# Sixteen experts: gate and up as seven block products instead of eight, on the two column halves of the array

## The chip, the cores and the metric

The kernel runs on one core of one Trainium2 chip. The metric is the device time of one launch in microseconds (us). Before the change the median of three runs is 3734.11 us (3731.77 to 3739.34).

The engines are TensorE (PE; its weight loads are listed as PEld), VectorE (DVE), ScalarE (ACT), GpSimd (POOL) and SyncE (SP), which here issues most DMAs. Data lie in SBUF (the one large tensor `arena`); matmuls write to PSUM (`ps`, eight banks of 512 words in each of 128 partitions).

## The reference, cut to what matters

The program computes a hybrid layer and then a second layer. The change is in the mixture of experts of the first layer:

```
def expert_choice_ffn(h, w_router, w_gate, w_up, w_down):
    def route_set(t):                       # t: 1024 tokens x 1024
        n = t.shape[0]
        cap = CAP_FACTOR * n // N_EXPERTS   # 128 tokens for each of 16 experts
        aff = jax.nn.softmax((t @ w_router).astype(jnp.float32), axis=-1)
        gate, idx = lax.top_k(aff.T, cap)
        xe = t[idx]
        hid = jax.nn.silu(jnp.einsum('ecd,edf->ecf', xe, w_gate)) * jnp.einsum('ecd,edf->ecf', xe, w_up)
        ye = jnp.einsum('ecf,efd->ecd', hid, w_down) * gate[..., None].astype(t.dtype)
        return jnp.zeros_like(t).at[idx.reshape(-1)].add(ye.reshape(-1, t.shape[-1]))
```

Each expert has three 1024 x 1024 matrices of float32, 12.6 MB together, and multiplies 128 tokens by each.

## The kernel before

The program is a row of stages with a barrier between them. `stage_choose` finds each expert's 128 tokens on VectorE and meanwhile loads the weights of expert 0. `stage_experts` (line 1757 on) does the experts one after the other. There is no scheduler: each engine has its instructions in the order of the code and waits on semaphores that the code names.

A weight matrix lies in two halves of four k blocks (`W[n][:, half]`, 2 MB each, loaded by one DMA), one buffer for each matrix. So a half of the next expert can be loaded as soon as TensorE has gone past that half (`load`, L1800).

TensorE's order for expert i (`body`, L1861) is: gate half 0, the eight transposes of the hidden rows of expert i-1 (`turn(hid)`), gate half 1, down of expert i-1 (two halves), the eight transposes of the tokens of expert i+1 (`turn(xe)`), up (two halves). A half is eight matmuls in the code, with 128 tokens as the stationary operand and 512 columns of weights as the moving one; a float32 matmul is two records in the trace. So an expert takes 96 records of 128x512 and 16 of 128x128, all on the full array, written `128*128` in the rows.

ScalarE copies the turned tokens out of PSUM (`rows_in`) and does silu (`gate`). VectorE multiplies (`hidden`, L1922), copies the turned hidden rows (L1928) and scales the result (L1936, `y`). GpSimd gathers the tokens (L1817, an indirect DMA from `h_scratch`) and adds `y` to the output rows (L1822, an indirect DMA to `x_scratch`). At the stage's start it also makes two products of gains for a later stage (L1829, L1831), which need `final_g` and `norm1_g_2`. SyncE issues the loads of these two (L1797, L1798) behind fourteen small loads for a later stage (L1787 to L1795).

A later stage, `stage_ffn_up` (L3210), already multiplies by seven block products on the full array; it has sums of operands on GpSimd (L3247 to L3250) and VectorE (L3315 to L3319).

## Time and profile before

| | |
|---|---|
| median of three runs | 3734.11 us |
| the profiled execution | 3731.01 us |
| its span, first to last instruction | 3729.1 us |
| TensorE busy | 3453.5 us (93%) |
| granted TensorE clock, mean | 0.963 |
| VectorE, ScalarE, GpSimd busy | 41%, 20%, 15% |
| mean HBM traffic | 114 GB/s |

All durations below come from that one profiled execution. PE busy counts a matmul to its modelled end, so two matmuls in a row overlap: the time that a stream of them costs is read from the distance of their starts. The clock is 1.00 at 2.4 GHz and 0.50 at 1.2 GHz. A row such as `PE L1845 MATMUL ... 128*128 128x512 f32 x48` merges 48 records; the first pair of numbers is the part of the array used (rows by columns), the second the shape of the result. In brackets stands how long the engine was idle before, and who ended it.

### The profile page before, as it was taken

How to read it: one execution, taken by the hardware profiler on the slowest of the kernel's cores; microseconds unless marked ns; L12 is line 12 of the kernel's file. 1: busy time of each engine (PE TensorE's matmuls, PEld its weight loads, DVE VectorE, ACT ScalarE, POOL GpSimd, SP SyncE). 2: the span in 40 equal slices, each digit the busy share in tenths (PEclk: the TensorE clock that was granted, in tenths of full speed). 3: DMA queues.
4: the chain of work that ended last, by engine and by line, in shares of the span. 5: the costliest groups of instructions: out<-in, count | busy, mean ns of one | idle time of the engine just before them, and what ended most of it. 6: DMA issues, size and time to landing. Idle time of an engine off the chain costs nothing. (4 is left out here: it accounts for less than half of the span.)

```text
span 3729.1 us, 32988 instructions
## 1 busy us (share of the span) xinstructions
PE 3453.5 (93%) x12660; PEld 1795.2 (48%) x12660; DVE 1524.8 (41%) x2809; ACT 748.1 (20%) x1454; POOL 559.9 (15%) x437
## 2 busy tenths in 40 slices
PE   6999999986889499999996989899999999999999
PEld 3445665545755244444443565345444444444444
DVE  3526853666343400000007658999322322211510
ACT  2004542442421000000002222233311101101000
POOL 0003420025610000000000020134200222221000
PEclk8999999998999699999997999999999999999999
DMA  6400001033332698888854033112223111110400
GB/s 245 146 23 23 1 2 34 24 106 91 82 137 95 242 339 315 315 316 322 318 189 165 0 59 96 51 38 91 95 70 115 34 45 45 45 35 28 152 23 34
DMA packets 199714, 427.59 MB, mean 115 GB/s; under 512 B 71449, under 2 KB 125881, under 8 KB 186753
## 3 DMA queue, kind: packets, MB, share of 16 engines
q1 hardware_dynamic: 190146, 394.18, 30.6%
q0 software_dynamic: 8272, 29.38, 2.6%
q8 instruction: 92, 1.51, 0.2%
q10 hardware_dynamic: 1152, 2.10, 0.2%
q14 instruction: 52, 0.43, 0.0%
HBM read 380.56 MB, written 43.88 MB: 114 GB/s over the span
## 5 line engine op out<-in xcount | busy, mean ns | idle before, releaser
L1845 PE MATMUL psum<-arena 128*128 128x512 f32 x1536 | 669.2, 594 | 2.5 <-DVE arena L1928 1.3
L3258 PE MATMUL psum<-arena 128*128 128x512 f32 x1232 | 534.1, 596 | 4.3 <-DVE arena L3316 3.3
L1845 PEld LDWEIGHTS psum<-arena 128*128 128x128 f32 x1536 | 289.0, 190 | 359.9 <-issue 356.9
L3258 PEld LDWEIGHTS psum<-arena 128*128 128x128 f32 x1232 | 235.5, 191 | 302.2 <-issue 296.8
L3412 PE MATMUL psum<-arena 128*128 128x512 f32 x528 | 229.6, 597 | 3.6 <-PEq L3231 3.6
L750 PE MATMUL psum<-arena 128*128 128x512 f32 (+1 forms) x512 | 198.3, 540 | 1.1 <-PEq L460 1.1
L2883 PE MATMUL psum<-arena 128*128 128x512 f32 x416 | 191.7, 604 | 3.7 <-ACT arena L2945 3.3
L2389 DVE TENSOR_SCALAR_CACHE_REDUCE arena<-arena 128x1024 f32<-128x1024 f32 (+2 forms) x192 | 173.6, 943 | 2.6 <-PEq L2462 0.8
L3412 PEld LDWEIGHTS psum<-arena 128*128 128x128 f32 x528 | 100.7, 191 | 132.5 <-issue 132.3
L2972 POOL TENSOR_SCALAR arena<-arena 128x128 f32<-128x128 f32 (+7 forms) x64 | 112.9, 1776 | 326.7 <-DVE arena L3008 326.7
L2133 PE MATMUL psum<-arena 128*128 128x512 f32 (+1 forms) x384 | 161.9, 581 | 0.0
L474 POOL TENSOR_TENSOR arena<-arena 128x1280 f32<-128x1280 f32 x32 | 92.6, 2894 | 423.9 <-DVE arena L589 423.9
L3327 DVE TENSOR_TENSOR arena<-arena,psum 128x512 f32<-128x512 f32 x44 | 30.3, 689 | 306.8 <-PE psum L3258 306.8
L1936 DVE SCALAR_TENSOR_TENSOR arena<-psum,arena 128x1024 f32<-128x1024 f32 x16 | 20.6, 1286 | 308.4 <-PE psum L1845 308.4
L750 PEld LDWEIGHTS psum<-arena 128*128 128x128 f32 x512 | 95.5, 189 | 91.0 <-issue 87.8
L355 PE MATMUL psum<-arena 128*128 128x512 f32 (+1 forms) x320 | 127.7, 554 | 1.9 <-PEq L154 1.9
L2133 PEld LDWEIGHTS psum<-arena 128*128 128x128 f32 x384 | 88.7, 233 | 68.5 <-issue 55.5
L3247 POOL TENSOR_TENSOR arena<-arena 128x512 f32<-128x512 f32 x22 | 28.6, 1299 | 611.0 <-PE psum L3258 370.8
L2883 PEld LDWEIGHTS psum<-arena 128*128 128x128 f32 x416 | 75.7, 192 | 92.2 <-issue 87.1
L1922 DVE TENSOR_TENSOR arena<-arena,psum 128x1024 f32<-128x1024 f32 x16 | 19.6, 1223 | 240.2 <-PE psum L1845 240.2
L1602 PE MATMUL psum<-arena 128*128 128x512 f32 x256 | 114.4, 602 | 2.2 <-PEq L1461 2.2
L3144 PE MATMUL psum<-arena 128*128 128x512 f32 x256 | 110.9, 592 | 2.4 <-PEq L3046 2.4
(513 smaller groups left out, 4635.0 us busy)
## 6 DMA issues: line engine op xcount, KB each, us to landing
arena<-in_w_gate_dram SPq DMA_DIRECT2D x32, 2048.0 KB, 7.4
arena<-in_w_up_dram SPq DMA_DIRECT2D x32, 2048.0 KB, 9.2
arena<-in_w_down_dram SPq DMA_DIRECT2D x32, 2048.0 KB, 8.2
arena<-in_w_mod_dram SPq DMA_DIRECT2D x12, 2048.0 KB, 9.7
arena<-gd_rows SPq DMA_DIRECT2D x56, 256.0 KB, 4.2
arena<-in_w_in_dram SPq DMA_DIRECT2D x22, 512.0 KB, 4.5
arena<-in_w_ffn_gate_dram SPq DMA_DIRECT2D x11, 1024.0 KB, 5.4
arena<-in_w_ffn_up_dram SPq DMA_DIRECT2D x11, 1024.0 KB, 5.3
```

Source lines behind the costliest of these rows:

```text
L355: ins = nc.tensor.matmul(e.ps[:, i % 4, 0:n], w[:, c % 2, k, m * P:(m + 1) * P], e.hT[:, k, s:s + n], start=(k == 0), stop=(k == KD - 1))
L474: nc.gpsimd.tensor_tensor(pr[:, i % SLOTS, 0], pr[:, i % SLOTS, 0], pr[:, i % SLOTS, 1], ALU.add).then_inc(s_comb, 1)
L750: ins = nc.tensor.matmul(e.ps[:, i % 4, 0:n], w[:, (m // 2) % 2, k, (m % 2) * P:(m % 2 + 1) * P], e.hT[:, k, s:s + n], start=(k == 0), sto ...
L1602: ins = nc.tensor.matmul(ps[:, 2 * (t % 2) + j, :], cat(k)[:, t * P:(t + 1) * P], w[:, k, j * 512:(j + 1) * 512], start=(k == 0), stop=(k ...
L1845: ins = nc.tensor.matmul(ps[:, banks + j, :], lhs[:, k], W[n][:, h, k % 4, j * 512:(j + 1) * 512], start=(k == 0), stop=(k == KD - 1))
L2133: ins = nc.tensor.matmul(ps[:, BANK(i), 0:n], lhs, w[:, (c + 2) % 3, k, 0:n], start=(k == 0), stop=(k == KD - 1))
L2389: ins = nc.vector.tensor_scalar(junk[j][:, 0:b.shape[-1]], b, cand.bitcast(F32)[:, j:j + 1], 0.0, ALU.is_ge, ALU.add, accum_out=count[:, j ...
L2883: ins = nc.tensor.matmul(ps[:, 7, :], wg[:, c % 2, k], hT[:, k, n * 512:(n + 1) * 512], start=(k == 0), stop=(k == KD - 1))
L2972: nc.gpsimd.tensor_scalar(v, v, sm[:, k % 2, 0, m:m + 1], None, ALU.mult).then_inc(s_nm, 1)
L3144: ins = nc.tensor.matmul(ps[:, 2 * (t % 2) + j, :], e.merged[:, k, t * P:(t + 1) * P], w[:, k, j * 512:(j + 1) * 512], start=(k == 0), sto ...
L3258: ins = nc.tensor.matmul(out(q), left[:, k], right[:, k], start=first and k == 0, stop=last and k == 3, skip_group_check=not first)
L3412: ins = nc.tensor.matmul(ps[:, bank + t, :], left(c)[:, tok(t)], right(c), start=first and c == 0, stop=c == KC - 1, skip_group_check=not ...
```

## The change

Gate and up are each multiplied as 2 x 2 blocks by the Winograd form of Strassen's scheme, which needs seven block products for eight. The tokens are split into two halves of 64 (`m`) and the contraction into the two weight halves (`h`); the weights' columns are split into quarters `b11, b12, b21, b22` that take four of every eight words. A product (`product`) has 64 tokens as the stationary operand, so it fills half of the array's columns; the code issues gate's matmul into PSUM partitions 0 to 63 and up's into 64 to 127, one after the other, for each of four k blocks. Down stays as it was.

The sums of weights (`t1` to `t4`, 128 x 2048 words each) are made by VectorE for gate and by GpSimd for up: `t3 = b22 - b12` in place of `b12` once both halves of the matrix are there (`third`), `t2 = t3 + b11` and `t1 = b22 - t2` after product P7, `t4 = b21 - t2` after P3. The semaphores `s_tg` and `s_tu` count them. VectorE makes four sums of tokens (128 x 256). Three partial results are put together by VectorE (`t[:, 0..2]`, six operations of 128 x 512), after ScalarE has copied four of them out of PSUM (`kept`); then TensorE transposes the four tiles (16 transposes, `tiles_turned`), and silu and the product with up are done on the transposed tiles. The loads of expert i+1 wait for the sums now, in the order gate 0, up 0, gate 1, up 1. `xe` has one buffer instead of two. (`...`: lines left out.)

```diff
+    t = A.take("tiles", 4, 512)
+    T = {n: [A.take(f"sum_{n}{m}", 4, 512) for m in range(3)] for n in ("gate", "up")}
...
+    xe = A.take("xe", D)
...
+    y = e.rows[:, 0]
...
+    X, Y, Z, V = range(4)
+    P1, P7, P2, P3, P6, P5, P4 = range(1, 8)
+    quarter = lambda n, h, c: W[n][:, h].rearrange("p k (m c) -> p k m c", c=KD)[:, :, :, 4 * c:4 * c + 4]
+    spread = lambda v: v.rearrange("p (m c) -> p m c", c=4)
+    b11, b12, b21, b22 = ({n: quarter(n, h, c) for n in ("gate", "up")} for h in range(2) for c in range(2))
+    t1, t2, t4 = ({n: T[n][m].rearrange("p k (m c) -> p k m c", c=4) for n in ("gate", "up")} for m in range(3))
+    t3 = b12
+    s3, s1, s2, s4 = (S[:, m] for m in range(4))
+    tokens = lambda b, h, m: xT[:, b, 4 * h:4 * h + 4, 64 * m:64 * m + 64]
...
+            def load(n, h, i):
+                sp.dma_start(W[n][:, h], src[n][bass.ds(i, 1), :, 4 * h:4 * h + 4, :].rearrange("a p k n -> p (a k) n")).then_inc(s_w[n][h], 16)
+
+            def body(i, b, first=False, second=False, last=False):
+                if not last:
+                    sp.wait_ge(s_tg, 4 * i + 2)
+                    load("gate", 0, i + 1)
+                    sp.wait_ge(s_tu, 4 * i + 2)
+                    load("up", 0, i + 1)
+                    sp.wait_ge(s_tg, 4 * i + 4)
+                    load("gate", 1, i + 1)
+                    sp.wait_ge(s_tu, 4 * i + 4)
+                    load("up", 1, i + 1)
+                if not first:
+                    for h in range(2):
+                        sp.wait_ge(s_d, 2 * i + h - 1)
+                        load("down", h, i)
+
+            experts(sp, body)
...
+            def third(i):
+                for h in range(2):
+                    pool.wait_ge(s_w["up"][h], 16 * (i + 1))
+                TT(t3["up"], b22["up"], b12["up"], ALU.subtract).then_inc(s_tu, 1)
...
-            gather(1)
...
             nc.gpsimd.tensor_tensor(e.rows[:, 1], e.rows[:, 1], e.rows[:, 1], ALU.mult).then_inc(e.s_gains, 1)
+            third(0)
+            pool.wait_ge(s_xt, 1)
+            gather(1)
             for i in range(NE):
-                if 1 <= i < NE - 1:
-                    gather(i + 1)
+                pool.wait_ge(s_mm, 7 * i + P7)
+                pool.wait_ge(s_tu, 4 * i + 1)
+                TT(t2["up"], t3["up"], b11["up"], ALU.add).then_inc(s_tu, 1)
+                pool.wait_ge(s_tu, 4 * i + 2)
+                TT(t1["up"], b22["up"], t2["up"], ALU.subtract).then_inc(s_tu, 1)
+                pool.wait_ge(s_mm, 7 * i + P3)
+                TT(t4["up"], b21["up"], t2["up"], ALU.subtract).then_inc(s_tu, 1)
                 if i:
+                    if i >= 2:
+                        pool.wait_ge(s_out, 16 * (i - 1))
                     scatter(i - 1)
+                if i + 2 < NE:
+                    pool.wait_ge(s_xt, i + 2)
+                    gather(i + 2)
+                if i + 1 < NE:
+                    third(i + 1)
+            pool.wait_ge(s_out, 16 * (NE - 1))
             scatter(NE - 1)
+            pool.wait_ge(s_out, 16 * NE)
...
+            def product(bank, left, right, first, last):
+                for k in range(4):
+                    for m, n in enumerate(("gate", "up")):
+                        ins = nc.tensor.matmul(spread(ps[64 * m:64 * m + 64, bank, :]), left[:, k], right[n][:, k], start=first and k == 0, stop=last and k == 3,
+                                               skip_group_check=not first)
+                ins.then_inc(s_mm, 1)
...
+            def tiles_turned():
+                for bank, pair in ((6, (t[:, 3], t[:, 1])), (4, (t[:, 0], t[:, 2]))):
+                    for c in range(2):
+                        for k in range(4):
+                            ins = nc.tensor.transpose(ps[:, bank + c, k * P:(k + 1) * P], pair[c].rearrange("p (m k) -> p k m", k=4)[:, k], e.ident)
+                    ins.then_inc(s_ct, 1)
...
+            def sums(i, n):
+                pe.wait_ge(s_tg, 4 * i + n)
+                pe.wait_ge(s_tu, 4 * i + n)
...
+                pe.wait_ge(s_xT, i + 1)
+                for n in ("gate", "up"):
+                    pe.wait_ge(s_w[n][0], 16 * (i + 1))
...
+                    pe.wait_ge(s_ev, 4 * i)
+                product(X, a11, b11, True, True)
                 if not first:
-                    pe.wait_ge(s_sg, i)
-                half("gate", 0, x, i, 0)
+                    pe.wait_ge(s_c, 6 * i)
+                    if not second:
+                        pe.wait_ge(s_y, i - 1)
+                    tiles_turned()
+                sums(i, 1)
+                pe.wait_ge(s_xs, 4 * i + 1)
+                product(Y, s3, t3, True, True)
+                for n in ("gate", "up"):
+                    pe.wait_ge(s_w[n][1], 16 * (i + 1))
+                pe.wait_ge(s_ev, 4 * i + 1)
+                product(X, a12, b21, False, True)
+                pe.wait_ge(s_xs, 4 * i + 4)
+                product(Z, s4, b22, True, True)
...
+                    down(i - 1)
+                sums(i, 2)
+                pe.wait_ge(s_ev, 4 * i + 2)
+                product(Y, s2, t2, False, True)
...
+                    pe.wait_ge(s_xe, 16 * (i + 2))
+                    turn()
+                sums(i, 4)
+                pe.wait_ge(s_ev, 4 * i + 4)
+                product(Z, s1, t1, False, True)
+                product(V, a22, t4, True, True)
...
+            def kept(i, n, tile, bank):
+                act.wait_ge(s_mm, 7 * i + n)
+                nc.scalar.activation(tile, ps[:, bank, :], ACT.Copy).then_inc(s_ev, 1)
...
+            def body(i, b, first=False, second=False, last=False):
...
+                    opened(i - 1, 0, not second)
+                    act.wait_ge(s_ct, 2 * i)
+                kept(i, P1, t[:, 0], X)
...
+                    opened(i - 1, 1, False)
+                kept(i, P7, t[:, 1], Y)
+                kept(i, P2, t[:, 3], X)
+                kept(i, P3, t[:, 2], Z)
+                if not last:
+                    rows_in(i + 1, 1 - b)
...
+            def hidden(i):
+                for m, bank in enumerate((6, 4)):
+                    v = hT[:, :, 64 * m:64 * m + 64]
+                    dve.wait_ge(s_sg, 2 * i + m + 1)
+                    TT(v, v, ps[:, bank:bank + 2, :].rearrange("p a (b c) -> p (a b) c", c=P)[:, :, 64:P], ALU.mult).then_inc(s_hT, 1)
...
+            def token_sums(i, b):
+                a11, a12, a21, a22 = (tokens(b, h, m) for m in range(2) for h in range(2))
+                dve.wait_ge(s_xT, i + 1)
+                TT(s3, a11, a21, ALU.subtract).then_inc(s_xs, 1)
+                TT(s1, a21, a22, ALU.add).then_inc(s_xs, 1)
+                dve.wait_ge(s_xs, 4 * i + 2)
+                TT(s2, s1, a11, ALU.subtract).then_inc(s_xs, 1)
+                dve.wait_ge(s_xs, 4 * i + 3)
+                TT(s4, a12, s2, ALU.subtract).then_inc(s_xs, 1)
+
+            def third(i):
+                for h in range(2):
+                    dve.wait_ge(s_w["gate"][h], 16 * (i + 1))
+                TT(t3["gate"], b22["gate"], b12["gate"], ALU.subtract).then_inc(s_tg, 1)
+
+            def body(i, b, first=False, second=False, last=False):
+                if not first:
+                    hidden(i - 1)
+                dve.wait_ge(s_mm, 7 * i + P7)
+                dve.wait_ge(s_tg, 4 * i + 1)
+                TT(t2["gate"], t3["gate"], b11["gate"], ALU.add).then_inc(s_tg, 1)
+                dve.wait_ge(s_tg, 4 * i + 2)
+                TT(t1["gate"], b22["gate"], t2["gate"], ALU.subtract).then_inc(s_tg, 1)
+                dve.wait_ge(s_mm, 7 * i + P3)
+                TT(t4["gate"], b21["gate"], t2["gate"], ALU.subtract).then_inc(s_tg, 1)
+                if not first:
+                    output(i - 1, second)
+                dve.wait_ge(s_ev, 4 * i + 4)
+                dve.wait_ge(s_mm, 7 * i + P6)
+                TT(t[:, 0], t[:, 0], ps[:, Y, :], ALU.add).then_inc(s_c, 1)
+                dve.wait_ge(s_c, 6 * i + 1)
+                TT(t[:, 1], t[:, 0], t[:, 1], ALU.subtract).then_inc(s_c, 1)
+                TT(t[:, 2], t[:, 0], t[:, 2], ALU.subtract).then_inc(s_c, 1)
+                dve.wait_ge(s_mm, 7 * i + P5)
+                dve.wait_ge(s_c, 6 * i + 2)
+                TT(t[:, 1], t[:, 1], ps[:, Z, :], ALU.add).then_inc(s_c, 1)
+                dve.wait_ge(s_c, 6 * i + 3)
+                TT(t[:, 2], t[:, 2], ps[:, Z, :], ALU.add).then_inc(s_c, 1)
+                if not last:
+                    token_sums(i + 1, 1 - b)
+                dve.wait_ge(s_mm, 7 * i + P4)
+                TT(t[:, 0], t[:, 0], ps[:, V, :], ALU.add).then_inc(s_c, 1)
+                if not last:
+                    third(i + 1)
```

Three places in the programs show what moves. First GpSimd at the stage's start. Before (L1817 is a gather, L1829 and L1831 the products of gains, L1822 a scatter):

```order
L1812 UNCONDITIONAL_BRANCH
L1817 DMA arena<-h_scratch,arena 128x1024 x2
L1829 TENSOR_TENSOR arena<-arena 128x1024
L1831 TENSOR_TENSOR arena<-arena 128x1024
L1817 DMA arena<-h_scratch,arena 128x1024
L1822 DMA x_scratch<-arena 1024x1024
```

And now (L1844 is the gather, L1859 and L1861 the gains, L1855 `third`, L1868, L1870 and L1872 `t2`, `t1` and `t4`):

```order
L1839 UNCONDITIONAL_BRANCH
L1844 DMA arena<-h_scratch,arena 128x1024
L1859 TENSOR_TENSOR arena<-arena 128x1024
L1861 TENSOR_TENSOR arena<-arena 128x1024
L1855 TENSOR_TENSOR arena<-arena 128x512x4
L1844 DMA arena<-h_scratch,arena 128x1024
L1868 TENSOR_TENSOR arena<-arena 128x2048
L1870 TENSOR_TENSOR arena<-arena 128x2048
L1872 TENSOR_TENSOR arena<-arena 128x2048
```

Expert 0's sum `t3` of up, for which TensorE's second product waits, now stands behind the products of gains, and the second gather behind it.

Second, TensorE from the stage's start. Before (L1851 are transposes, L1845 matmuls; counts are of the code, two records each for L1845):

```order
L1839 UNCONDITIONAL_BRANCH
L1851 MATMUL psum<-arena 128x128 x8
L1845 MATMUL psum<-arena 128x512 x16
L1851 MATMUL psum<-arena 128x128 x8
L1845 MATMUL psum<-arena 128x512 x24
L1851 MATMUL psum<-arena 128x128 x8
L1845 MATMUL psum<-arena 128x512 x24
```

And now (L1897 turns tokens, L1891 is `product`, 8 a product, L1904 turns the tiles, L1913 is down):

```order
L1886 UNCONDITIONAL_BRANCH
L1897 MATMUL psum<-arena 128x128 x8
L1891 MATMUL psum<-arena 64x512 x40
L1897 MATMUL psum<-arena 128x128 x8
L1891 MATMUL psum<-arena 64x512 x24
L1904 MATMUL psum<-arena 128x128 x16
L1891 MATMUL psum<-arena 64x512 x24
L1913 MATMUL psum<-arena 128x512 x16
L1891 MATMUL psum<-arena 64x512 x8
```

An expert has 56 matmuls on half the columns where it had 32 on all of them, 24 transposes where it had 16, and goes between the two uses of the array six times.

Third, SyncE behind the two loads of gains. Before (L1803 loads weights):

```order
L1798 DMA arena<-in_norm_g_dram 128x1024
L1803 DMA arena<-in_w_gate_dram 128x4096 x2
L1803 DMA arena<-in_w_up_dram 128x4096 x2
L1806 UNCONDITIONAL_BRANCH
L1806 ISA
```

And now (L1820 loads weights):

```order
L1817 DMA arena<-in_norm_g_dram 128x1024
L1820 DMA arena<-in_w_gate_dram 128x4096
L1820 DMA arena<-in_w_up_dram 128x4096
L1820 DMA arena<-in_w_gate_dram 128x4096
L1820 DMA arena<-in_w_up_dram 128x4096
```

The halves of gate and up alternate, and each has a wait for a sum before it.

## Rows read from the trace of the kernel before

**Rows 1.** Page, part 5: line, engine, shapes, count | busy us, mean ns | idle before.

```profile
L1845 PE MATMUL psum<-arena 128*128 128x512 f32 x1536 | 669.2, 594 | 2.5 <-DVE arena L1928 1.3
```

**Rows 2.** Windows: stretch, us, busy by engine, clock, DMA share, GB/s.

```profile
1200.00:1265.00 65.00, 10.45 (x44) 8.83 (x44) 41.63 (x101) 3.96 (x7) 3.14 (x5) 0.50 0.61 234
...
1438.00:1481.00 43.00, 43.00 (x113) 19.86 (x113) 3.79 (x4) 2.05 (x2) 2.56 (x2) 1.00 0.86 317
```

**Rows 3.** Timeline, steady experts: start us, us, engine, line.

```profile
1560.93 1.06 PE L1851 MATMUL psum<-arena 128*128 128x128 f32 x8
...
1561.83 20.80 PE L1845 MATMUL psum<-arena 128*128 128x512 f32 x48
...
1582.83 1.29 DVE L1936 SCALAR_TENSOR_TENSOR arena<-psum,arena 128x1024 f32<-128x1024 f32 x1 [19.52 <-PE psum L1845]
```

**Rows 4.** Timeline of VectorE, one expert later.

```profile
1625.87 1.29 DVE L1936 SCALAR_TENSOR_TENSOR arena<-psum,arena 128x1024 f32<-128x1024 f32 x1 [19.52 <-PE psum L1845]
```

**Rows 5.** Timeline of TensorE, a stage that uses column halves (L2903).

```profile
2669.17 0.88 PE L2903 MATMUL psum<-arena 128*64 128x128 f32 x12
2669.98 0.55 PE L2893 MATMUL psum<-arena 128*128 128x128 f32 x3
```

**Rows 6.** Timeline of TensorE, a stage that uses row halves (L485).

```profile
298.92 5.00 PE L485 MATMUL psum<-arena 64*128 64x256 f32 x12 [3.25 <-ACT arena L536]
...
447.25 2.42 PE L485 MATMUL psum<-arena 64*128 64x512 f32 x10
449.60 0.44 PE L501 MATMUL psum<-arena 128*128 128x128 f32 x2
```

**Rows 7.** Timeline, start of the experts.

```profile
1261.60 12.05 SPq L1792 DMA_DIRECT2D arena<-in_B_re_dram  x2
1262.28 1.97 PE L1851 MATMUL psum<-arena 128*128 128x128 f32 x8 [8.97 <-DMA arena<-h_scratch,arena]
...
1265.37 15.57 PE L1845 MATMUL psum<-arena 128*128 128x512 f32 x32 [1.11 <-ACT arena L1899]
...
1280.78 1.05 PE L1851 MATMUL psum<-arena 128*128 128x128 f32 x8
...
1281.66 21.12 PE L1845 MATMUL psum<-arena 128*128 128x512 f32 x48
...
1284.26 0.44 SPq L1798 DMA_DIRECT2D arena<-in_norm_g_dram  x1
...
1290.71 2.34 POOL L1829 TENSOR_TENSOR arena<-arena 128x1024 f32<-128x1024 f32 x1 [31.43 <-DMA arena<-in_norm_g_dram]
1293.13 1.89 POOL L1831 TENSOR_TENSOR arena<-arena 128x1024 f32<-128x1024 f32 x1
```

**Rows 8.** Groups, sums on GpSimd of 512 and 1280 words.

```profile
L3247 POOL TENSOR_TENSOR arena<-arena 128x512 f32<-128x512 f32 x22 | 28.6, 1299 | 611.0 <-PE psum L3258 370.8 <-issue 240.1
...
L474 POOL TENSOR_TENSOR arena<-arena 128x1280 f32<-128x1280 f32 x32 | 92.6, 2894 | 423.9 <-DVE arena L589 423.9
```

**Rows 9.** Groups by form, VectorE, 1985 to 2120 us.

```profile
L2235 DVE TENSOR_TENSOR arena<-arena 128x2048 f32<-128x2048 f32 x1 | 2.3, 2294 | 0.0
...
L2235 DVE TENSOR_TENSOR arena<-arena 128x256 f32<-128x256 f32 x2 | 0.9, 427 | 0.1
```

**Rows 10.** Timeline, sums on GpSimd and VectorE at the same time.

```profile
2922.81 1.59 POOL L3248 TENSOR_TENSOR arena<-arena 128x512 f32<-128x512 f32 x1
2923.32 1.63 DVE L3316 TENSOR_TENSOR arena<-arena 128x512 f32<-128x512 f32 x1
2924.48 1.59 POOL L3249 TENSOR_TENSOR arena<-arena 128x512 f32<-128x512 f32 x1
...
2929.05 0.69 DVE L3319 TENSOR_TENSOR arena<-arena 128x512 f32<-128x512 f32 x1
```

**Rows 11.** Page, part 6: issue, count, KB each, median us to landing.

```profile
arena<-in_w_gate_dram SPq DMA_DIRECT2D x32, 2048.0 KB, 7.4
```

**Rows 12.** Timeline, the last expert's end.

```profile
1960.47 1.28 DVE L1936 SCALAR_TENSOR_TENSOR arena<-psum,arena 128x1024 f32<-128x1024 f32 x1 [15.69 <-PE psum L1845]
```

More of the change, by code:

```diff
@@ L1915, in _ @@
+            rows_in(0, 0)
+            experts(act, body)
+            opened(NE - 1, 0, True)
+            opened(NE - 1, 1, False)
         @block.vector
         def _(dve):
[L1917 to L1922 removed]
+            TT = nc.vector.tensor_tensor
@@ L1947, in stage_between @@
+            third(0)
+            token_sums(0, 0)
+            experts(dve, body)
+            hidden(NE - 1)
+            output(NE - 1, False)
+    A.give(*("w_" + n for n in names), "tiles", *(f"sum_{n}{m}" for n in ("gate", "up") for m in range(3)), "xe", "xT", "x_sums", "hidT", "gcol", "idxT", "gateT")
 def stage_between(e):
```

140 lines of the change are left out of this document (45 added, 95 removed).

## The prediction

> **What bounds the kernel now.** I read the page first: TensorE is busy 93% of the span, and L1845, the experts' matmuls, is its costliest line [rows 1]. Then the windows by stage: while the experts run, TensorE is busy all of the time at clock 1.00, GpSimd 2.6 of 43 us and VectorE 3.8, and the DMAs move 317 GB/s [rows 2]. The timeline of steady experts has no gap: 48 records of 128x512 take 20.80 us, which is (20.80 - 0.59) / 47 = 0.430 us from start to start, and 8 transposes go by in 1561.83 - 1560.93 = 0.90 us, 0.112 each [rows 3]. An expert is then 96 x 0.430 + 16 x 0.112 = 43.1 us, and VectorE's row L1936 does come back after 1625.87 - 1582.83 = 43.04 [rows 3, 4]. So a steady expert is bound by TensorE's stream. The stage's start is another case: GpSimd's products of gains wait until 1290.71 for two loads that SyncE issues only at 1284, after it was held up by the small loads, but nobody waits for them [rows 7].
>
> **TensorE, steady.** A product is 16 records (8 matmuls, two records each). The trace does not show 64-column matmuls of 512 words. It shows column halves at 128 words: 12 records of L2903 need 2669.98 - 2669.17 = 0.81 us to the next line's start, where 12 in a row on the whole array would need 12 x 0.112 = 1.34 [rows 5]. That is six pairs at 0.12 (or at 0.112 with 0.1 for the change of use). Row halves at 512 words do the same: 8 records of 512 and 2 of 256 in 449.60 - 447.25 = 2.35 us, that is four pairs and two halves, 4 x 0.43 + 2 x 0.215 = 2.15, and 0.2 for the change of use and a weight load [rows 6]. I take 0.43 a pair and 0.09 a change; the ends are 0.46 (0.12 / 0.112 x 0.43) and 0.86, no overlap at all. So: seven products 7 x 8 x 0.43 = 24.1; down 32 x 0.43 = 13.8; 24 transposes 2.7; six changes 0.5. Together 41.1 us for 43.04, 2.0 less.
>
> The Trainium skill ("TensorE: Matmul & The Clock Gate", section "Measured speedup vs the span model") gives 2.38 times for three column tiles of 512 words. By that efficiency a pair would cost 1.26 single matmuls, and as an estimate this change would lose some 100 us in all; rows 5 and 6 are much nearer to 1, and I go by them.
>
> A moving operand in runs of four words out of eight (`b11`, `b12`, `b21`, `b22` in four products) is shown by no row; I take it as free, and at the worst it is twice the time of these four, 13.8 us an expert. The skill ("SBUF — State Buffer", section "Door 1: The DMA port swizzle", its note on cachelines) says that reads run at full rate where at least two fall into each 16-byte line, and four float32 words fill one; by that it would be free. No run here shows it so far.
>
> **GpSimd and VectorE, steady.** A sum of weights is 2048 words. On VectorE it is 2.29 us [rows 9]. GpSimd has 1.30 for 512 and 2.89 for 1280 words [rows 8], 2.08 ns a word, so 4.5 us; the ends are 3.8 (twice L1831's 1.89) and 5.2 (four times 1.30) [rows 7, 8]. They don't run side by side: with GpSimd's sums going, VectorE's sum of 512 words takes 1.63 us for 0.69 and GpSimd's 1.59, and the two make one of each every 1.67 us, the sum less 0.3 [rows 10]. So `t2`, `t1`, `t4` of gate and up take 3 x (2.29 + 4.5 - 0.3) = 19.5 us. This makes a second loop beside TensorE: P7 (3.44 + 0.2), the six sums 19.5, the load of up half 1, which SyncE issues last, 7.4 [rows 11], `t3` of up 4.5; then VectorE, blocked until that is done, four token sums (0.43 each, rows 9), the last partial 0.7, `t3` of gate 2.3; and the next P7. Sum 39.7, with ten hand-overs of 0.05 about 40.2. TensorE's own loop is 41.1: the cover is 0.9 us. The scatter of 0.5 MB can meet that load and cost it up to a microsecond; I take the period as 41.2, between 41.1 and 43.1 (GpSimd at 5.2 us puts 2.8 into the loop).
>
> The other new work is hidden while that cover holds: ScalarE's copies and silu lie behind products; VectorE's partials wait for P6 and P5 and are needed after the next P1; the down loads come after up's but are wanted 14 us into the next expert; six loads of 2 MB are what was moved before. VectorE's `y` is queued behind `t4`, and the scatter behind GpSimd's `t4`, but no one waits soon for either.
>
> **The stage's start.** P1 of expert 0 starts at 1265.4 as before, at the half clock [rows 2, 7]: 32 records took 1280.78 - 1265.37 = 15.4 for 13.8 there, 1.65 more, so P1 ends at 1270.5. P7 waits for `t3` of up, which stands on GpSimd behind the gains: 1293.13 + 1.89 = 1295.0 [rows 7], plus 4.5 gives 1299.6. TensorE has idled 29 us. After an idle time of 3.25 us, 12 records of L485 (8 of 512 and 4 of 256 words; the row names one form) took 5.00 us, where 4 x 0.43 + 4 x 0.215 = 2.6 is the full pace [rows 6]; so a restart is cold, and I add 1.8 us to each. P7 ends at 1304.9, P2, P3, P6 and the transposes at 1316.2 (none of expert 0's products has a down beside it). P5 needs `t4` of up: 1304.9 + 0.2 + 19.5 = 1324.7. P5 and P4, cold again, end at 1333.5. Before, expert 1 began at 1281.66 + 32 x 0.43 = 1295.4 [rows 7]. The loss is 38.1 us. In expert 1 it goes on: up half 1, issued at 1324.7, lands at 1332.1, `t3` of up ends at 1336.6, VectorE's row of small sums and `t3` of gate at 1341.3, while TensorE is ready at 1333.5 + 3.4 + 1.9 = 1338.9: 2.3 us more.
>
> **The end.** Before, from 1295.4 + 15 x 43.04 = 1941.0 to L1936 at 1960.47 is 19.5 us [rows 12]. Now: last partial 0.9, 16 transposes 1.8, silu and product 1.4, down 13.8, 0.3 to `y`, less the turn of tokens that the last expert lacks, 1.0: 17.2. I count 2 us gained.
>
> **Sum.** 38.1 + 2.3 - 2.0 - 15 x (43.04 - 41.2) = +10.8. On the profiled execution's 3731.0 that is 3742; its time is 3.1 under the median of the runs shown, 3734.1, so for that median 3745.
>
> **Rivals.** (a) The sums are cheap: GpSimd needs 3.8 us, or the pairs of sums overlap more than in rows 10. Then four sums at the start end 3 us sooner or more and the period is TensorE's 41.1: 38.1 - 4 + 2.3 - 2 - 29.1 = +5, and +2 with both: no change, 3738. For it: L1831's 1.89. Against it: L1829's 2.34 for 1024 words lies on the line through rows 8, only L1831 lies below, and rows 10 are the very same operations. (b) The loop of sums and loads binds: GpSimd at 5 us or the last load at 9. Period 43.1, nothing saved in 15 experts, +40 and the start 2 more: 3776. For it: a cover of only 0.9 us over nine steps; against it: a sum may cost 4.7 us before it binds, and the straight line through rows 8 gives 4.5. (c) The other side, faster: the gain loads land sooner than 1290.7 now that no weight loads follow them closely. TensorE's wait of 29 us falls with it; at 11 us sooner all is even, at 20 us sooner it is 3745 - 20 = 3725. Against it: the loads are issued at 1284 behind small loads that the change leaves alone, so 6 us is all there is to win. (d) The halves don't overlap at 512 words: 24 us an expert, 4120; with half the overlap 3930; the strided operand at twice its time is 13.8 us an expert, 3965.
>
> **Chances.** The forecast 0.47, (a) 0.23, (b) 0.20, (c) 0.04, (d) 0.06. A measurement of this kernel tells 0.2% (7.5 us) from no change. A quarter of the forecast's own range, +4 to +20, lies under it. So slower 0.35 + 0.20 + 0.06 = 0.61, no change 0.12 + 0.23 = 0.35 and faster 0.04; I move 0.03 from no change to faster, for a gain that I have not seen: 0.32 and 0.07. The range takes (a), the forecast and (b): 3735 to 3782.
>
> **What would show it.** Right: L1891 in pairs with 0.43 us between pairs; TensorE idle from about 1270.5 to 1299.6 with GpSimd named as the releaser, and again some 8 us before expert 0's sixth product; expert to expert 41.1 to 41.4; VectorE's sums of weights at 2.3 us alone and over 4 us when GpSimd's are going. Wrong: P7 waiting in each expert (then (b), and the last sum's and last load's times say which), a first wait under 20 us (c), or pairs above 0.46 us (d).

## The result and the profile after

| | kernel before | changed kernel |
|---|---|---|
| median, us (4 runs each, one chip) | 3732.94 (3731.02 to 3739.34) | 3797.89 (3796.42 to 3799.05) |
| ratio to before | 1 | 1.0171, 95% interval 1.0153 to 1.0188 |
| span of the profiled execution | 3729.1 | 3796.9 |
| mean granted TensorE clock | 0.963 | 0.954 |

The changed kernel is 65 us slower. The forecast was 3745 with a range up to 3782: the sign was right, the size was wrong by 53 us. Of all executions counted in this document three ran far slower than the rest (6989 and 9292 us of the kernel before, 9091 of the one with all sums on VectorE); the ratios leave them out, and they move no median by more than 0.5 us.

The page of the changed kernel, parts 5 and 6 (part 5: line, engine, shapes, count | busy us, mean ns | idle before; part 6: issue, count, KB, us to landing):

```profile
L1891 PE MATMUL psum<-arena 128*64 128x512 f32 x1792 | 417.0, 619 | 65.6 <-issue 42.7
...
L2040 DVE TENSOR_TENSOR arena<-arena 128x2048 f32<-128x2048 f32 x16 | 77.6, 4850 | 88.3 <-PE psum L1891 88.3
...
arena<-in_w_gate_dram SPq DMA_DIRECT2D x32, 2048.0 KB, 7.3
arena<-in_w_up_dram SPq DMA_DIRECT2D x32, 2048.0 KB, 11.7
arena<-in_w_down_dram SPq DMA_DIRECT2D x32, 2048.0 KB, 19.9
```

The first row answers to [rows 1]: its 669 us of busy time, which held gate, up and down, are now 417 of products and 224 of down (L1913), and 65.6 us of waiting came where 2.5 had been. VectorE's sum of 2048 words, L2040, is at 4.85 us on average where [rows 9] had 2.29. The gate loads land as they did [rows 11]. Up's and down's take 11.7 and 19.9 us, where the page of the kernel before had 9.2 and 8.2:

```profile
arena<-in_w_up_dram SPq DMA_DIRECT2D x32, 2048.0 KB, 9.2
```

Steady experts, the timeline of TensorE (start us, us, line; L1891 products, L1897 turned tokens, L1904 turned tiles, L1913 down), which answers to [rows 3]:

```profile
1597.42 1.16 PE L1897 MATMUL psum<-arena 128*128 128x128 f32 x8
1598.51 10.71 PE L1891 MATMUL psum<-arena 128*64 128x512 f32 x48
1609.14 2.20 PE L1904 MATMUL psum<-arena 128*128 128x128 f32 x16
1613.55 11.03 PE L1891 MATMUL psum<-arena 128*64 128x512 f32 x48 [2.20 <-DVE arena L2033]
1624.51 14.03 PE L1913 MATMUL psum<-arena 128*128 128x512 f32 x32
...
1642.06 1.16 PE L1897 MATMUL psum<-arena 128*128 128x128 f32 x8
```

From one turn of tokens to the next it is 44.64 us, where a steady expert took 43.04. A wait of 2.2 us stands before P7, and it ends with L2033, VectorE's `t3` of gate. Without that wait an expert takes 42.4 us. Now the three queues that lead to it, in the same stretch, GpSimd first (L1855 is `t3`, L1868, L1870 and L1872 are `t2`, `t1`, `t4` of up):

```profile
1605.84 5.51 POOL L1855 TENSOR_TENSOR arena<-arena 128x2048 f32<-128x2048 f32 x1 [6.01 <-DMA arena<-in_w_up_dram]
1617.47 3.60 POOL L1868 TENSOR_TENSOR arena<-arena 128x2048 f32<-128x2048 f32 x1 [6.12 <-PE psum L1891]
1621.14 6.57 POOL L1870 TENSOR_TENSOR arena<-arena 128x2048 f32<-128x2048 f32 x1
1627.67 6.66 POOL L1872 TENSOR_TENSOR arena<-arena 128x2048 f32<-128x2048 f32 x1
1640.80 1.58 POOL L1849 DMA_INDIRECT x_scratch<-arena  x1 [6.47 <-DVE arena L2017]
1643.50 0.98 POOL L1844 DMA_INDIRECT arena<-h_scratch,arena  x1 [1.11 <-PE psum L1897]
1650.58 5.54 POOL L1855 TENSOR_TENSOR arena<-arena 128x2048 f32<-128x2048 f32 x1 [6.10 <-DMA arena<-in_w_up_dram]
```

SyncE, which issues the loads (first the halves 0, then the halves 1 of the next expert):

```profile
1623.39 0.33 SPq L1820 DMA_DIRECT2D arena<-in_w_gate_dram  x1
1623.83 0.37 SPq L1820 DMA_DIRECT2D arena<-in_w_up_dram  x1
1636.65 0.33 SPq L1820 DMA_DIRECT2D arena<-in_w_gate_dram  x1
1637.08 0.38 SPq L1820 DMA_DIRECT2D arena<-in_w_up_dram  x1
1637.64 1.26 SPq L1820 DMA_DIRECT2D arena<-in_w_down_dram  x2
```

VectorE (L2040, L2042, L2044 are `t2`, `t1`, `t4` of gate):

```profile
1617.51 5.71 DVE L2040 TENSOR_TENSOR arena<-arena 128x2048 f32<-128x2048 f32 x1 [2.82 <-PE psum L1891]
1623.25 6.61 DVE L2042 TENSOR_TENSOR arena<-arena 128x2048 f32<-128x2048 f32 x1
1629.79 6.70 DVE L2044 TENSOR_TENSOR arena<-arena 128x2048 f32<-128x2048 f32 x1
...
1650.91 7.36 DVE L2033 TENSOR_TENSOR arena<-arena 128x2048 f32<-128x2048 f32 x1
```

This is the loop that binds. P7 starts at 1613.55, the sums at 1617.5 (4.0 us). All six are done at 1636.5 (19.0). GpSimd's next `t3` starts when up half 1 has landed, at 1650.58 (14.1). VectorE's `t3` ends at 1658.27 (7.7), and the next P7 follows. The sum of the rounded terms is 44.8 us. Up half 1 was issued at 1637.08, 0.4 us behind gate half 1, and took 13.5 us.

Up half 0 was issued at 1623.83, also 0.4 us behind gate's half, and landed after 11.7 us. The difference of 1.8 us is not the queue's order. While half 1 is under way, GpSimd issues the scatter (1640.80) and the gather (1643.50), 0.5 MB each; while half 0 is, it issues neither. That these two cost the 1.8 us fits, and no run took them away.

The start, which answers to [rows 7]: TensorE, then GpSimd (L1859 and L1861 are the products of gains).

```profile
1269.08 6.57 PE L1891 MATMUL psum<-arena 128*64 128x512 f32 x16 [1.11 <-ACT arena L1968]
1303.13 17.29 PE L1891 MATMUL psum<-arena 128*64 128x512 f32 x64 [27.48 <-issue]
1320.36 1.15 PE L1897 MATMUL psum<-arena 128*128 128x128 f32 x8
1328.90 12.70 PE L1891 MATMUL psum<-arena 128*64 128x512 f32 x48 [7.39 <-issue]
```

```profile
1293.38 2.33 POOL L1859 TENSOR_TENSOR arena<-arena 128x1024 f32<-128x1024 f32 x1 [31.13 <-DMA arena<-in_norm_g_dram]
...
1297.64 5.39 POOL L1855 TENSOR_TENSOR arena<-arena 128x2048 f32<-128x2048 f32 x1
```

The stage's matmuls start 3.7 us later than in the profile of before (P1 of expert 0 at 1269.08 for 1265.37). In the traces of this case the turn of tokens before P1 starts anywhere between 1261 and 1267, and what follows the last `y` takes 1762 to 1772 us, with no pattern by kernel, so I count neither. TensorE's wait of 27.48 us ends 0.1 us after `t3` of up (1297.64 + 5.39 = 1303.03). The row names no releaser (`<-issue`), so the times and the order of the code say what it waited for, and the second experiment tests it. The wait of 7.39 us likewise ends 0.1 us after `t4` of up.

### The profile page after: what moved, and what is told of

It reads as the page before. It is cut to its first block and busy times, and to the rows that moved or that the text cites. A ratio compares the mean times of both kernels' runs of the same rounds, so it can differ in the third digit from the quotient of the medians.

```text
span 3796.9 us, 35475 instructions
## 1 busy us (share of the span) xinstructions
PE 3462.0 (91%) x13556; PEld 1755.4 (46%) x13556; DVE 1971.4 (52%) x3033; ACT 787.7 (21%) x1534; POOL 930.3 (25%) x501
## 5 line engine op out<-in xcount | busy, mean ns | idle before, releaser
L3384 PE MATMUL psum<-arena 128*128 128x512 f32 x1232 | 534.2, 596 | 4.3 <-DVE arena L3442 3.3
L1891 PE MATMUL psum<-arena 128*64 128x512 f32 x1792 | 417.0, 619 | 65.6 <-issue 42.7
L3384 PEld LDWEIGHTS psum<-arena 128*128 128x128 f32 x1232 | 235.5, 191 | 302.4 <-issue 296.9
L1891 PEld LDWEIGHTS psum<-arena 128*64 128x64 f32 x1792 | 129.1, 138 | 328.1 <-issue 300.9
L3538 PE MATMUL psum<-arena 128*128 128x512 f32 x528 | 229.7, 597 | 3.6 <-PEq L3357 3.6
L1913 PE MATMUL psum<-arena 128*128 128x512 f32 x512 | 224.4, 594 | 1.4 <-DVE arena L2007 1.4
L3009 PE MATMUL psum<-arena 128*128 128x512 f32 x416 | 191.4, 603 | 3.7 <-ACT arena L3071 3.3
L3538 PEld LDWEIGHTS psum<-arena 128*128 128x128 f32 x528 | 100.8, 191 | 132.5 <-issue 132.3
L1913 PEld LDWEIGHTS psum<-arena 128*128 128x128 f32 x512 | 95.5, 189 | 130.2 <-issue 128.5
L750 PEld LDWEIGHTS psum<-arena 128*128 128x128 f32 x512 | 96.7, 191 | 91.3 <-issue 87.7
L2040 DVE TENSOR_TENSOR arena<-arena 128x2048 f32<-128x2048 f32 x16 | 77.6, 4850 | 88.3 <-PE psum L1891 88.3
L2259 PEld LDWEIGHTS psum<-arena 128*128 128x128 f32 x384 | 88.5, 233 | 68.1 <-issue 55.1
L3009 PEld LDWEIGHTS psum<-arena 128*128 128x128 f32 x416 | 75.6, 192 | 92.5 <-issue 87.4
L1602 PE MATMUL psum<-arena 128*128 128x512 f32 x256 | 115.4, 606 | 2.2 <-PEq L1461 2.2
## 6 DMA issues: line engine op xcount, KB each, us to landing
arena<-in_w_up_dram SPq DMA_DIRECT2D x32, 2048.0 KB, 11.7
arena<-in_w_down_dram SPq DMA_DIRECT2D x32, 2048.0 KB, 19.9
```

The source lines that it names most:

```text
L750: ins = nc.tensor.matmul(e.ps[:, i % 4, 0:n], w[:, (m // 2) % 2, k, (m % 2) * P:(m % 2 + 1) * P], e.hT[:, k, s:s + n], start=(k == 0), sto ...
L1602: ins = nc.tensor.matmul(ps[:, 2 * (t % 2) + j, :], cat(k)[:, t * P:(t + 1) * P], w[:, k, j * 512:(j + 1) * 512], start=(k == 0), stop=(k ...
L1891: ins = nc.tensor.matmul(spread(ps[64 * m:64 * m + 64, bank, :]), left[:, k], right[n][:, k], start=first and k == 0, stop=last and k == 3 ...
L1913: ins = nc.tensor.matmul(ps[:, 4 + j, :], hT[:, k], W["down"][:, h, k % 4, j * 512:(j + 1) * 512], start=(k == 0), stop=(k == KD - 1))
L2259: ins = nc.tensor.matmul(ps[:, BANK(i), 0:n], lhs, w[:, (c + 2) % 3, k, 0:n], start=(k == 0), stop=(k == KD - 1))
L3009: ins = nc.tensor.matmul(ps[:, 7, :], wg[:, c % 2, k], hT[:, k, n * 512:(n + 1) * 512], start=(k == 0), stop=(k == KD - 1))
```

## The experiments

Every kernel was timed against the kernel before, on the same chip within one group (medians of before: 3733.07, 3733.53, 3734.47). The changed kernel itself was timed once, with the result; differences from it are between groups, whose medians of before lie within 1.6 us (3732.94 to 3734.47). "Period" is the distance between the outputs `y` of two steady experts.

**Down loads held back.** Only SyncE's order changes:

```
                 if not first:
+                    if not last:
+                        sp.wait_ge(s_w["up"][1], 16 * (i + 2))
                     for h in range(2):
                         sp.wait_ge(s_d, 2 * i + h - 1)
```

> One edit on the changed kernel: SyncE issues an expert's two down loads only when up half 1 of the next expert has landed. Theory L (the second loop binds: P7 3.6 us, six sums 19.0, the load of up half 1 13.7 from issue to landing, the two third sums 7.7; sum 44.0 for a period of 44.7): up half 1 then shares the DMA engines with gate half 1 alone (4 MB at some 420 GB/s and 1 to 2 us of latency, an estimate from the load's trace) and lands after 10.5 to 11 us, the loop falls to 41 and TensorE's own loop of 42.4 binds; 14 periods x 2.3 = 32 us less, 3765 (3760 to 3772), and P7 waits under 0.5 us in steady experts. Theory T (TensorE's stream itself is what became longer, by the strided operand and the changes of use): the wait moves only, time within 3 us of 3798. Theory S (the collision of the two third sums alone): DVE's third stays at 7.2 us, and the period falls by less than 1 us: 3785 or more.

Measured: 3798.14 us (3788.96 to 3799.45), ratio 1.0176 (1.016 to 1.0193), no difference from the changed kernel. SyncE and GpSimd in that trace:

```profile
1636.16 0.33 SPq L1820 DMA_DIRECT2D arena<-in_w_gate_dram  x1
1636.59 0.38 SPq L1820 DMA_DIRECT2D arena<-in_w_up_dram  x1
1650.24 0.81 SPq L1820 DMA_DIRECT2D arena<-in_w_down_dram  x2
```

```profile
1650.22 5.51 POOL L1857 TENSOR_TENSOR arena<-arena 128x2048 f32<-128x2048 f32 x1 [6.24 <-DMA arena<-in_w_up_dram]
```

The down loads start some 13 us later and up half 1 still takes 13.6 us. My first theory of why the load is late (the down loads behind it share the engines) fell. What is behind a load in the queue does not slow it here. My second theory was that what is ahead of it does, and that is gate half 1; the run with the two exchanged, below, tests that.

**Third sum ahead of the gains.** `third(0)` moves above the wait for the gain loads on GpSimd, the two products of gains to the top of expert 1.

> One edit on the changed kernel: GpSimd does the third sum of expert 0 before its two products of gains, which move to the top of expert 1. My theory of the start: TensorE's idle 27.5 us before P7 of expert 0 is the wait for the gain loads. P7 then starts right behind P1 (about 1273 where it was 1303), the six sums run from 1276 to 1296, P5 of expert 0 waits for the last of them, and expert 1 starts near 1304 instead of 1337: 33 us less, of which the gains give back up to 4 in expert 1. Expected 3797.9 - 29 = 3769 (3764 to 3775), steady period unchanged at 44.7. Rival: the sums of expert 0 are slowed by the loads then in flight, and the wait moves to P5 whole: under 15 us gained, 3783 or more.

Measured: 3775.88 us (3769.52 to 3779.03), ratio 1.0118 (1.0102 to 1.0135): 22 us of the 29 expected. TensorE ran P1 to P6 of expert 0 without a gap, and then (the first wait is for `t4` of up, as before):

```profile
1295.45 8.99 PE L1892 MATMUL psum<-arena 128*64 128x512 f32 x32 [7.42 <-issue]
1306.72 3.82 PE L1892 MATMUL psum<-arena 128*64 128x512 f32 x16 [2.28 <-DMA arena<-in_w_up_dram]
...
1321.88 13.33 PE L1892 MATMUL psum<-arena 128*64 128x512 f32 x48 [9.19 <-issue]
```

The 27 us were the gains. But two new waits, 2.3 and 9.2 us, stand in expert 1, both for weights. SyncE could issue its loads only from 1289.46 on, behind the small loads, and until now TensorE's own delay had covered that. Three halves went out within 1.5 us, and up half 1, issued at 1295.38 as soon as its sums were done, landed 21 us later (GpSimd's `t3` waits for it until 1316.39, and TensorE's P7 until 1321.88).

**Both thirds on VectorE.** GpSimd keeps `t2`, `t1`, `t4` of up; in VectorE's `third`:

```
+    for h in range(2):
+        dve.wait_ge(s_w["up"][h], 16 * (i + 1))
+    TT(t3["up"], b22["up"], b12["up"], ALU.subtract).then_inc(s_tu, 1)
```

> One edit on the changed kernel: the third sum of up moves from GpSimd to VectorE, behind the third sum of gate; GpSimd keeps t2, t1, t4 of up. Theory L with the sum of terms: the pair of thirds costs 2.3 + 2.3 = 4.6 us behind the landing instead of 7.7, the loop is 44.0 - 3.1 = 41, TensorE's 42.4 binds: 32 us less in 14 periods. At the start P7 of expert 0 no longer waits for the gains but t2 of up does (until about 1297), so P5 of expert 0 starts near 1315 instead of 1329: 14 us less. Together 3752 (3745 to 3762). Theory T (TensorE's stream): only the start's 14 us, 3784. Theory 'load only' (the thirds are hidden, only the late load counts): period falls by under 1 us, 3770 to 3784.

Measured: 3742.55 us (3738.73 to 3744.52), ratio 1.0023 (1.0013 to 1.0033). The period is 42.37 us and P7 of a steady expert never waits. It is 9 us better than expected, 5 of them at the start, where the first `y` came 19 us earlier for 14. Up half 1 still lands 13.2 us behind its issue (at 1604.20). So the loop of sums and loads binds the changed kernel, and taking 3 us out of it is enough for TensorE to bind, even with the late load.

**Contiguous blocks.** A block is a run of 512 words; hidden units are numbered by halves, and down's rows are loaded in that order:

```
-    quarter = lambda n, h, c: W[n][:, h].rearrange("p k (m c) -> p k m c", c=KD)[:, :, :, 4 * c:4 * c + 4]
...
+    quarter = lambda n, h, c: W[n][:, h, :, 512 * c:512 * c + 512]
...
+    halves = e.in_["w_down"][0].rearrange("e (h p k) n -> e p h k n", h=2, k=4)
```

> One edit on the changed kernel: the blocks b11, b12, b21, b22 are contiguous runs of 512 words of a row (the hidden units are numbered by halves, and down's rows are loaded in that order), so no product reads runs of four words out of eight. Pairs of products on those blocks take 0.451 us from start to start in the changed kernel, those on the sums' tiles 0.431. If the stride is the cause, all pairs take 0.431 and the four products of an expert save 32 x 0.020 = 0.65 us. Theory L (the loop of sums and loads binds, not TensorE): nearly nothing of it reaches the time, P7 only waits longer (3.0 instead of 2.6 us): 3797 (3793 to 3800). Theory T (TensorE binds): 15 x 0.65 = 10 us less, 3788. If the 0.451 comes from VectorE's or GpSimd's reads beside it and not from the stride, it stays.

Measured: 3784.16 us (3781.92 to 3785.64), ratio 1.0139 (1.0122 to 1.0156): 14 us less, where one theory said 1 and the other 10. The trace says why neither fits. TensorE still waits, so it does not bind:

```profile
1647.21 2.21 PE L1907 MATMUL psum<-arena 128*128 128x128 f32 x16
1651.29 10.52 PE L1894 MATMUL psum<-arena 128*64 128x512 f32 x48 [1.86 <-issue]
```

The period fell from 44.66 to 43.99 us on average (most are 43.63 and five 45.33) because the loop of sums got shorter too: VectorE's `t3` now begins before GpSimd's and costs 2.29 us for 7.3. The price of the stride is plain: 48 records take 10.52 us for 11.03, that is 0.02 a pair.

The five long periods are TensorE's clock. In each of them P7, P2 and P3 take 12.22 us and not 10.52, behind the same wait of 1.86:

```profile
1605.96 12.22 PE L1894 MATMUL psum<-arena 128*64 128x512 f32 x48 [1.86 <-issue]
```

The granted clock was 0.55 in the first 3.6 us of that row, near the 1.2 GHz level, and 1.00 in the first 3.6 us of the row at 1651.29. The two periods of 46.3 us in the changed kernel are the same thing: the rows at 1567.30 and 1837.01, behind waits of 2.27 and 2.19 us, take 12.64 us for 11.03, at clock 0.67 and 0.66 in their first 3.6 us where the row at 1613.50 has 1.00.

**Up half 1 ahead of gate half 1.** SyncE issues the two in the other order, nothing else.

> One edit on the changed kernel: SyncE issues the load of up half 1 before that of gate half 1 instead of behind it. Theory Q (the queue serves its loads in order; up half 1 took 13.7 us because gate half 1 is ahead of it, and that load ends the loop of sums): up half 1 lands 7.3 us after its issue, GpSimd's third sum starts near 7.5 us behind the last sum instead of 14.1, VectorE's third follows at about 12.5 and costs 2.3 us; the loop falls from 44.7 to about 39, TensorE's 42.4 binds, P7 waits under 0.3 us: 14 x 2.3 = 32 us less than 3798, 3766 (3758 to 3773). Rival (the down loads or the scatter share the engines evenly with it): up half 1 still lands after 12 us or more and the time stays within 5 us of 3798.

Measured: 3760.77 us (3758.26 to 3763.57), ratio 1.007 (1.0053 to 1.0087): 37 us less than the changed kernel. In the two traces 32.5 us of it lie between P1 of expert 0 and the last `y`, 32.0 of them in the fourteen periods; the rest is outside the stage. SyncE and GpSimd:

```profile
1576.37 0.33 SPq L1820 DMA_DIRECT2D arena<-in_w_up_dram  x1
1578.39 0.33 SPq L1820 DMA_DIRECT2D arena<-in_w_gate_dram  x1
```

```profile
1586.37 5.46 POOL L1855 TENSOR_TENSOR arena<-arena 128x2048 f32<-128x2048 f32 x1
```

GpSimd's `t3` no longer waits for a load at all; it follows its own gather, 10.0 us behind the issue where it was 13.5, and VectorE's `t3`, no longer beside it, takes 2.29 us for 7.4. Both come from the one exchange, and this run does not part them. The period is 42.38 and P7 doesn't wait. So the load ahead in the queue is what cost the steady experts their time, and the down loads, issued right behind here too, are not.

**Contiguous and up first.**

> The changed kernel with up half 1 loaded before gate half 1 (3760.8 with that alone, period 42.37, no wait before P7) and with contiguous blocks. Now that TensorE binds, the 32 pairs of an expert at 0.431 instead of 0.451 us must show in the time: period 42.38 - 0.67 = 41.7, 3760.8 - 10 = 3751 (3747 to 3755). Rival: the loop of sums (19.9 with GpSimd's sum at 4.5 us on contiguous blocks, and the loads) binds again and takes it: P7 waits, time above 3756.

Measured: 3751.31 us (3747.43 to 3752.42), ratio 1.004 (1.0027 to 1.0053); period 41.70. With TensorE binding, the stride's 0.67 us an expert shows whole.

**All sums on VectorE**, none on GpSimd, the gains at expert 1:

> The changed kernel with all eight sums of an expert's weights on VectorE (2.29 us each alone) and none on GpSimd, whose products of gains move to the top of expert 1. Theory K (two-input operations of VectorE and GpSimd exclude each other, so GpSimd's share costs more than it takes off): the six sums take 6 x 2.3 = 13.8 us instead of 19.0, every one at 2.3 us; the period is TensorE's 42.4; at the start TensorE waits for t4 until about 1290 and in expert 1 for up half 1, issued at 1290 behind the small loads, until about 1316. Expected 3797.9 - 33 (steady) - 24 (start) = 3740 (3732 to 3746), under the kernel with the thirds alone on VectorE (3742.6). Rival (VectorE becomes the bound with 18.4 us of sums and some 7 of other work): a period above 42.5 and time above 3750.

Measured: 3738.7 us (3734.44 to 3740.4, but for the one execution named above), ratio 1.0013 (1.0003 to 1.0023). The six sums of an expert on VectorE, in pairs:

```profile
1622.92 4.50 DVE L2031 TENSOR_TENSOR arena<-arena 128x2048 f32<-128x2048 f32 x2 [1.97 <-PE psum L1877]
1627.33 4.49 DVE L2034 TENSOR_TENSOR arena<-arena 128x2048 f32<-128x2048 f32 x2
1631.73 4.49 DVE L2037 TENSOR_TENSOR arena<-arena 128x2048 f32<-128x2048 f32 x2
```

They take 13.3 us, where the two engines together took 19.0. For these six sums GpSimd's help was a loss. The two hardly run side by side: VectorE's sum of 2.29 us took 6.61 beside GpSimd's, which takes 4.63 alone, and 2.29 + 4.63 is 6.9.

**The small loads later**, with the third sum first: the small parameters and the gains go behind the weight loads that SyncE issues while expert 0 runs (they are expert 1's weights), the products of gains to expert 3.

> The changed kernel with GpSimd's third sum of expert 0 ahead of its products of gains (which go to the top of expert 3), and with SyncE's small loads and the gains' loads issued behind expert 0's weight loads instead of ahead of them. In the kernel with only the first edit (3775.9) TensorE still waited 2.3 us for up half 0 and 9.2 us for up half 1 of expert 1, whose loads SyncE issued only from 1289.5 on, behind the small ones. Theory: both waits are the small loads'; up half 0 has landed before P1 of expert 1, up half 1 lands by 1309, P7 of expert 1 starts near 1317 instead of 1322: 5 us less, 3771 (3765 to 3776). Rival: the small loads in flight slow expert 1's or 2's weight loads as much: 3776 or more.

Measured: 3770.46 us (3767.84 to 3775.34), ratio 1.01 (1.0083 to 1.0117). The size was as expected, and the reason was not. P7 of expert 1 came 11.7 us earlier (1.8 of it because P1 of expert 0 did), for 5, and expert 2 then waited:

```profile
1310.21 12.60 PE L1895 MATMUL psum<-arena 128*64 128x512 f32 x48 [2.53 <-DVE arena L2037]
...
1364.74 5.44 PE L1895 MATMUL psum<-arena 128*64 128x512 f32 x16 [10.52 <-issue]
```

The small loads keep SyncE from 1293.5 to 1329.5 here, as they did from 1258.9 to 1288.0 in the changed kernel, and expert 2's weights came behind them: the wait was moved on by one expert.

**All together**, that is all sums on VectorE, contiguous blocks, late gains and late small loads:

> All edits that have shown an effect or should: all sums on VectorE, contiguous blocks, the gains' products at expert 3, the small loads behind expert 0's weight loads. TensorE's loop is 42.37 - 0.67 = 41.7 us and binds; the loop of sums is 3.6 + 13.8 + 14 + 4.6 = 36. Start: P5 of expert 0 at about 1290, P7 of expert 1 waits some 5 us for up half 1 and the thirds until 1308. Against the kernel before: first expert's output 8 us later, 14 periods x 1.34 = 19 us saved, 4 us saved at the end: 3733 - 15 = 3718 (3708 to 3728). Rival: VectorE's queue (two sums per matrix before P5, partials behind them) makes TensorE wait in each expert: above 3730.

Measured: 3730.28 us (3727.96 to 3736.18), ratio 0.9992 (0.9983 to 1.0002), short of the expected 3718 by the same wait: 55.0 us from the first `y` to the second.

**Small loads in two parts**, otherwise the same:

```
-                if not first:
+                if first:
+                    small_a()
+                else:
...
+                if second:
+                    small_b()
```

`small_a` holds A and log_dt, issued while expert 0 runs; `small_b` holds B, C and the gains, issued while expert 1 runs.

> The kernel with all sums on VectorE, contiguous blocks and late gains (3730.3), with SyncE's small loads in two parts: A and log_dt behind expert 0's weight loads, B, C and the gains behind expert 1's. In one piece they kept SyncE until 1328, so that expert 2's weights came late (55.0 us from output 0 to output 1 for 41.7). Theory: B and C (22 us of issue) fit between expert 1's last load and expert 2's first, that period goes to some 42, and the time to 3730.3 - 13 = 3717 (3713 to 3723), faster than the kernel before by 0.4%. Rival: the small transfers themselves slow the weight loads behind them: a period above 48 stays, 3723 or more.

Measured: 3719.84 us (3719.02 to 3723.37), ratio 0.9961 (0.9948 to 0.9974). This one is faster than both kernels, 0.4% faster than the kernel before. The first two periods are 44.2 and 42.9, all others 41.7, and TensorE has no wait in those:

```profile
1712.39 3.66 PE L1887 MATMUL psum<-arena 128*64 128x512 f32 x16
1715.99 1.16 PE L1893 MATMUL psum<-arena 128*128 128x128 f32 x8
1717.07 10.53 PE L1887 MATMUL psum<-arena 128*64 128x512 f32 x48
1727.54 2.21 PE L1900 MATMUL psum<-arena 128*128 128x128 f32 x16
1729.68 10.53 PE L1887 MATMUL psum<-arena 128*64 128x512 f32 x48
```

**The same with shared sums**, up's on GpSimd again and up half 1 loaded first:

> The same as the kernel with the small loads in two parts, but with the sums shared as in the changed kernel (up on GpSimd, gate on VectorE), GpSimd's first third sum ahead of the gains and up half 1 loaded before gate half 1. Theory: in steady experts the sharing costs nothing any more (loop 3.6 + 19.9 + 15 = 38.5 under TensorE's 41.7), but at the start P5 of expert 0 waits 6 us longer for t4, and up half 1 of expert 1 is issued 6 us later: 3717 + 7 = 3724 (3720 to 3730). Rival (GpSimd's sums slow the steady experts too): periods above 42, 3735 or more.

Measured: 3729.17 us (3723.94 to 3735.99), ratio 0.9988 (0.9979 to 0.9997). The steady periods are 41.7 as well. So sharing the sums costs a steady expert nothing once TensorE binds; it costs 9 us in all, at the start, where P5 of expert 0 waits 8.3 us and P7 of expert 2 5.4.

## Why the prediction was wrong, point by point

- **The start: right.** Said: P1 of expert 1 at 1333.5, a loss of 38.1, and 2.3 more in expert 1. Its first `y` was then due at 1366.1 by the same steps (P7 at 1341.3, 10.7 of products, 14.1 to `y`). Measured 1370.60, less the 3.7 by which this stage began late: 1366.9. The wait for the gains was 27.5 us for 29, the second 7.4 for 8.5. Only the sign "GpSimd named as the releaser" did not come: both rows say `issue`.
- **The sums: right in sum.** 19.0 us for 19.5. The terms under it were less good: GpSimd's sum is not 4.5 us but 3.6 to 5.4 by its layout (last section).
- **The load of up half 1: the step that failed.** "The load of up half 1, which SyncE issues last, 7.4 [rows 11]." 7.4 us is gate's landing, with nothing ahead of it; the same page already had 9.2 for up's loads, which alone would have made the loop 42.0 and longer than TensorE's 41.1. Here the sums of gate and up end together, so gate half 1 and up half 1 are issued 0.4 us apart, and the second takes 13.5. From the last sum to GpSimd's `t3` it is 14.1 us for 7.4, 6.7 more in the second loop. Some 4.3 of that go with the load ahead, since up half 0 lands after 11.7, and some 1.8 with the scatter and the gather, for which I had allowed "up to a microsecond"; the exchange shows that the load ahead counts, the split is read from the two halves of up, and no run tests the second part. 1.5 us came back in what follows the landing, where VectorE's `t3` ends 7.7 us behind it for 9.2. P7 with its hand-over took 4.0 for 3.64, the sums 19.0 for 19.5, and the 0.5 of hand-overs lies inside these stretches: 40.2 + 6.7 - 1.5 + 0.4 - 0.5 - 0.5 is 44.8, and the periods are 44.66 on average. The cover of 0.9 us was gone, and the period is the loop's. Exchanging the two loads gave back 37 us, 32 of them in the periods; taking the down loads away from behind it gave nothing. I had even written that the last load at 9 us would bind, and priced that rival at 43.1 us a period; the likely value of the load was never worked out from what is ahead of it.
- **TensorE's stream: 1.3 us an expert too cheap.** 42.38 for 41.1. The overlap of the halves was right. The stride, taken as free, costs 0.67 (contiguous blocks: 42.38 to 41.70, and 9.5 us of time). The other 0.6 lies in the changes of use and the transposes: 16 transposes of the tiles take 2.14 to the start of the next line (1727.54 to 1729.68 above), against 1.79 at 0.112; no run parts it further. Two halves at 512 words measured 10.53 / 24 = 0.439 for a pair, ends and change included, against 0.43 for one whole matmul, so for two halves the overlap is near whole. By its note on cachelines the Trainium skill ("SBUF — State Buffer", section "Door 1: The DMA port swizzle") had spoken for a stride that is free; the runs show 5% on a product whose moving operand comes in runs of four words out of eight, and they decide. The Trainium skill's 2.38 for three column tiles ("TensorE: Matmul & The Clock Gate", section "Measured speedup vs the span model") would, as an estimate, make a pair as dear as 1.26 single matmuls; the measured pair is 1.02 of one.
- **The end: right.** From the fifteenth `y` to the last 28.9 us, where the steps give 28.4.
- **The sum.** Start +0.8, fourteen periods 14 x (44.66 - 41.2) = +48.4, end +0.5: 49.7 of the 52.9 us by which the forecast fell short. Of the 48.4, 14 x (44.66 - 42.38) = 31.9 are the load's and 16.5 TensorE's; in the 31.9 are 2 x 1.6 us of TensorE at a lower clock behind the wait. The last 3 us lie outside these stretches, in stages that the change leaves alone.
- **The rivals.** (b) is what happened, with another price: I let it cost 43.1 us a period, because I took the load at 9 at the worst. (a) and (c) did not happen. Of (d), the stride came at 5% of four products and not at twice their time; its 4120 and 3930 are counted from 3734 and not from the forecast, and are some 10 us too low.

What stays open: why the clock falls behind some of the waits of 1.9 to 2.3 us before P7 and not behind others of the same length. It does not happen in the steady experts of the kernels whose P7 doesn't wait. That the scatter and the gather are the 1.8 us between up's two halves is not tested either.

## What to carry to other kernels

When a loop closes over a transfer, price that transfer by what is ahead of it in its own queue at that moment, not by the row of a load that goes alone; and if two loads become due together, issue first the one with the longer work behind it. Before two-input sums are shared between VectorE and GpSimd, add their times instead of taking the longer: one engine alone did in 13.3 us what both did in 19.0. And each wait that goes uncovers the next: here the gains, then the small loads in SyncE's queue, then the same loads one expert later, before a faster version stood.
